# A decoder layer with product-key experts: how the indices of the first expert rows are made

## The reference, cut to what matters

```python
def reference(x, mem, ...):                       # x: 1 x 256 x 1024, float32
    h = rmsnorm(x, norm_mix);   x = x + hybrid_mixer(h, ...)            # 16 heads of attention, w_in, w_out
    h = rmsnorm(x, norm_xattn); x = x + memory_cross_attention(h, ...)  # w_xq, w_xk, w_xv, w_xo
    h = rmsnorm(x, norm_ffn);   x = x + peer_ffn(h, ...)
    return rmsnorm(x, norm_final)

def one_chunk(xc):                                # inside peer_ffn: 128 tokens
    qr = (xc @ w_query).reshape(C, PEER_HEADS, 2, half)        # 8 heads
    s1 = einsum('chd,hnd->chn', qr[:, :, 0], sub_keys_1)       # 128 keys a side
    s2 = einsum('chd,hnd->chn', qr[:, :, 1], sub_keys_2)
    v1, i1 = top_k(s1, 16);  v2, i2 = top_k(s2, 16)
    cand = v1[..., :, None] + v2[..., None, :]                 # 16 x 16 sums
    top_s, pos = top_k(cand, 16)
    eidx = take_along_axis(i1 * 128 + i2, pos)                 # 16 experts per head
    g = softmax(top_s)
    a = gelu(einsum('cd,chkd->chk', xc, expert_down[eidx]))
    return einsum('chk,chkd->cd', g * a, expert_up[eidx])
```

## Time and profile before

| | us |
|---|---|
| median of 3 runs | 937.75 (935.33 to 939.22) |
| the profiled execution's own time | 927.9 |
| its span, first to last instruction | 926.1 |
| PE busy | 815.2 |
| DVE busy | 556.4 |
| ACT busy | 443.6 |
| POOL busy | 242.6 |
| bytes moved by DMA | 316.33 MB |

### The profile page before, as it was taken

The page is one execution under the profiler, slowest core; times in us unless marked ns, Lnnn a source line. Parts: engine busy times, 40 slices in busy tenths (PEclk is TensorE's granted clock), DMA queues, the critical chain, the costliest instruction groups (busy, mean ns, idle before and its releaser), DMA issues.

```text
span 926.1 us, 9462 instructions
## 1 busy us (share of the span) xinstructions
PE 815.2 (88%) x3195; PEld 457.9 (49%) x3195; DVE 556.4 (60%) x1345; ACT 443.6 (48%) x1088; POOL 242.6 (26%) x267
## 2 busy tenths in 40 slices
PE   7999999999989899888898999977877788787875
PEld 7999986687555365343343455432322222232322
DVE  5555333213456776777767758776766766676543
ACT  5435564324134645664546545464453545445343
POOL 0000000000023333334334333433333333333430
PEclk9999999999999999999999999999999999999999
DMA  9896632061099999999999999999999999999995
GB/s 334 227 312 244 205 115 91 1 230 44 1 371 413 415 422 419 413 416 421 419 409 421 421 413 417 418 410 416 421 422 421 422 421 416 421 408 423 409 422 218
DMA packets 64339, 316.33 MB, mean 342 GB/s; under 512 B 7907, under 2 KB 12068, under 8 KB 31524
## 3 DMA queue, kind: packets, MB, share of 16 engines
q0 software_dynamic: 36864, 268.45, 70.1%
q1 hardware_dynamic: 26348, 45.70, 13.9%
q10 hardware_dynamic: 1080, 1.59, 1.1%
HBM read 313.10 MB, written 2.62 MB: 341 GB/s over the span
## 4 chain that ended last, share of the span: by engine, by line
PE 53%; DMA 29%; ACT 10%; DVE 6%; issue 2%; POOL 0%; SPq 0%; POOLq 0%
DMA qkvb<-in_expert_rows,expert_idx 22%; PE y L1311 14%; PE v_bank L1311 8%; DMA spare<-in_expert_rows,expert_idx 6%; PE h_psum L1087 5%; PE v_bank L1077 5%; PE a_bank L1077 4%; PE a_bank L1087 4%; PE v_bank L1087 3%; DVE qkvb L1017 3%; PE h_psum L1077 3%; ACT L722 2%; PE v_bank L1176 2%; ACT diag L729 2%; PE y L1197 1%
## 5 line engine op out<-in xcount | busy, mean ns | idle before, releaser
L554 POOL DMA_INDIRECT qkvb<-in_expert_rows,expert_idx x172 | 162.1, 942 | 530.3 <-DVE expert_idx L1000 256.8
L722 ACT ACTIVATE gelu<-dots,stat 128x1 f32<-128x1 f32 x256 | 75.1, 293 | 309.3 <-DVE dots L1017 308.7
L1311 PE MATMUL v_bank<-qkvb,diag 128*128 128x512 f32 x344 | 171.8, 630 | 45.5 <-ACT diag L729 45.5
L1311 PE MATMUL y<-qkvb,diag 128*128 128x512 f32 x344 | 161.8, 607 | 21.2 <-ACT diag L729 21.2
L1017 DVE CUSTOM_DVE_ANT_0 qkvb<-a_bank,qkvb 128x1024 f32<-128x1024 f32 x86 | 105.3, 1224 | 74.1 <-DMA qkvb<-in_expert_rows,expert_idx 74.1
L1017 DVE CUSTOM_DVE_ANT_0 qkvb<-h_psum,qkvb 128x1024 f32<-128x1024 f32 x86 | 105.1, 1223 | 60.3 <-DMA qkvb<-in_expert_rows,expert_idx 60.3
L1311 PEld LDWEIGHTS v_bank<-qkvb,diag 128*128 128x128 f32 x344 | 61.4, 194 | 155.4 <-ACT diag L729 105.1
L554 POOL DMA_INDIRECT spare<-in_expert_rows,expert_idx x84 | 79.0, 941 | 132.5 <-PE y L1311 65.9
L1311 PEld LDWEIGHTS y<-qkvb,diag 128*128 128x128 f32 x344 | 62.1, 191 | 100.6 <-issue 56.5
L729 ACT ACTIVATE diag<-ident,wgt 128x128 f32<-128x128 f32 x256 | 102.7, 401 | 8.3
L1311 PE MATMUL v_bank<-spare,diag 128*128 128x512 f32 x168 | 85.1, 635 | 20.5 <-ACT diag L729 20.5
(11 more groups left out here) (204 smaller groups left out, 1142.8 us busy)
## 6 DMA issues: line engine op xcount, KB each, us to landing
weights<-in_w_in SPq DMA_DIRECT2D x5, 2048.0 KB, 33.2
weights<-in_w_xk SPq DMA_DIRECT2D x2, 2048.0 KB, 17.4
weights<-in_w_xv SPq DMA_DIRECT2D x2, 2048.0 KB, 10.7
weights<-in_w_out SPq DMA_DIRECT2D x2, 2048.0 KB, 8.9
weights<-in_w_xq SPq DMA_DIRECT2D x2, 2048.0 KB, 8.5
weights<-in_w_xo SPq DMA_DIRECT2D x2, 2048.0 KB, 12.1
weights<-in_w_peer_query SPq DMA_DIRECT2D x2, 2048.0 KB, 16.5
qkvb<-in_expert_rows,expert_idx POOLq DMA_INDIRECT x172, 9.9
```

What stands on the lines that cost most here:

```text
L554: pool.indirect_dma_start(ROWS[n % NS], None, expert_rows, bass.IndirectOffsetOnAxis(ap=IDX[:, H % 3, k:k + 1], axis=0))\
L722: nc.scalar.activation(gel[:, i:i + 1], dots[:, i:i + 1], ACT.Gelu, scale=rms("root_p", n // SPT)).then_inc(gelu_done, 1)
L1311: ins = nc.tensor.matmul(YP[t][:, b * BLK:(b + 1) * BLK], diag[:, i, :], ROWS[i][:, D + b * BLK:D + (b + 1) * BLK], start=False, stop=n % ...
```

## The change

It has five parts. (1) The norm weights of the last norm are a sixth load into `grow`, and `pT` transposes `X[0]` itself; DVE multiplies by the weight columns as the transpose leaves its bank. `xg` and ACT's copy are gone. (2) A quarter of `wout(1, 1)` that stood between the two transposes stands behind the scores now, and the two `y_start` products change place. (3) `top_part` reads scores where they lie, without a copy, for all 16 heads. (4) For head 0 the places of the first eight sums are turned into indices before the other eight are looked for (`FIRST_TOP`), and the reciprocal of the norm moves behind them. (5) POOL waits for the first eight indices before row tile 0 and for the others before row tile 8. Token tile 1 gets part 1 too.

```diff
-    main += [("xo", 0, 0), ("oT", 1, 0), ("xg", 0, 0), ("oT", 1, 1), ("xo", 0, 1), ("xg", 0, 1), ("pT", 0, 0)]
-    main += rest[1][:1] + [("square_p", 0, 0), ("pT", 0, 1), ("start", 0, 0), ("wq_first", 0, 0), ("y_start", 0, 0),
-                           ("sc_first", 0, 0), ("sc_first", 0, 1), ("root_p", 0, 0), ("top", 0, 0), ("y_start", 0, 1)]
-    main += rest[1][1:] + [("wq", 0, 0), ("sc", 0, 0), ("sc", 0, 1)] + rest[0]
+    main += [("xo", 0, 0), ("oT", 1, 0), ("oT", 1, 1), ("xo", 0, 1), ("pT", 0, 0), ("y_start", 0, 0), ("square_p", 0, 0),
+             ("pT", 0, 1), ("start", 0, 0), ("wq_first", 0, 0), ("sc_first", 0, 0), ("sc_first", 0, 1),
+             ("y_start", 0, 1), ("root_p", 0, 0), ("top", 0, 0)]
+    main += rest[1] + [("wq", 0, 0), ("sc", 0, 0), ("sc", 0, 1)] + rest[0]
...
+    CHOICE = ("pairs", "ones", "picks", "experts")
+    FIRST_TOP = TOP[:8] + tuple("first " + part for part in CHOICE) + TOP[8:11] + tuple(
+        "last " + part for part in CHOICE) + TOP[15:]
...
-                if k == 0:
-                    pool.wait_ge(idx_ready, H + 1)
+                if n == 0:
+                    pool.wait_ge(idx_ready, 1)
+                elif n == 8 or n > 8 and k == 0:
+                    pool.wait_ge(idx_ready, H + 2)
...
-            for r in (4, 0, 3):
+            for r in (4, 0, 3, 5):
                 load_gain(act, r)
...
-                elif name == "pT":
-                    src = job(key)
-                    act.copy(HT[t][:, 4 * i:4 * i + 4, :], src[:, :].rearrange("p (c x) -> p c x", c=4))\
-                        .then_inc(a_free, 1)
...
+                    if name == "wq_first":
+                        act.wait_ge(sum_done, norm_n[0])
...
-                    for part in TOP:
-                        if part == "sums":
+                    for part in FIRST_TOP:
+                        if part == "sums out":
                             rstd(("root_p", 0, 0))
                         top_part(part, 0)
...
-                elif name == "xg":
-                    own = slice(i * BLK, (i + 1) * BLK)
-                    dve.wait_ge(ld_gffn, 16)
-                    dve.wait_ge(*freed(("xo", t, i)))
-                    nc.vector.tensor_tensor(HTpage[t][:, own], X[t][:, own], gffn[:, own], ALU.mult)\
-                        .then_inc(xs_done, 1)
+                elif name == "pT":
+                    gained(key, i, HT[t], 32)
...
+                side = [sc[:, s, :] if lo else scores[:, s * NKEY:(s + 1) * NKEY] for s in range(2)]
                 if part in ("keys", "more keys"):
                     if lo == 0:
                         top_n[0] = 0
-                        after(t_mark(nc.vector.tensor_copy(sc[:, :, :].rearrange("p a x -> p (a x)"), scores)))
...
                 elif name == "pT":
-                    pe.wait_ge(xs_done, XN[("xg", t, i)])
-                    transposes(key, HTpage[t], i)
+                    pe.wait_ge(*freed(("xo", t, i)))
+                    transposes(key, X[t], i)
                 elif name == "y_start":
-                    pe.wait_ge(v_free, VN[("xo", t, 1)] + 1)
+                    pe.wait_ge(*freed(("xo", t, i)))
```

More of the change, by code:

```diff
@@ L189, in hybrid_layer @@
               (122, ("sc", 1, 2)), (123, ("sc", 1, 3))]
-    OWN = ("root_x", "rstd_x", "xnorm", "xg", "square_p", "root_p", "rstd_p")
+    OWN = ("root_x", "rstd_x", "xnorm", "square_p", "root_p", "rstd_p")
     def after_slot(n, products):
@@ L284, in hybrid_layer @@
         skT = sb("subkeys_t", [P, PH, NKEY])
-        grow = PT[0:32, 0, 0:P]
-        gcol = sb("gain_cols", [P, 32])
+        grow = PT[0:40, 0, 0:P]
+        gcol = sb("gain_cols", [P, 40])
         wf = sb("w_forget", [P, KC, NH])
@@ L776, in gained @@
                                         src[:, :].rearrange("p (c x) -> p c x", c=4),
-                                        gain, ALU.mult).then_inc(v_free, 1)
+                                        gain, ALU.mult).then_inc(freed(key)[0], 1)
             def step(name, t, i):
@@ L939, in top_part @@
                 lo = 8 if part.startswith("more") else 0
+                ks = slice(0, PK)
+                if part.startswith(("first", "last")):
+                    ks = slice(0, 8) if part.startswith("first") else slice(8, PK)
+                    part = part.split()[1]
+                nk = ks.stop - ks.start
+                side = [sc[:, s, :] if lo else scores[:, s * NKEY:(s + 1) * NKEY] for s in range(2)]
                 if part in ("keys", "more keys"):
@@ L946, in top_part @@
                     for s in range(2):
-                        ins = nc.vector.max(kv[:, s, lo:lo + 8], sc[:, s, :])
+                        ins = nc.vector.max(kv[:, s, lo:lo + 8], side[s])
                         top_mark["keys", s] = t_mark(ins)
@@ L981, in top_part @@
                     after(top_mark["sum places"])
-                    t_mark(nc.vector.tensor_scalar(pab[:, 0, :], pos[:, :], 4, None, ALU.logical_shift_right))
-                    after(t_mark(nc.vector.tensor_scalar(pab[:, 1, :], pos[:, :], 15, None, ALU.bitwise_and)))
-                    top_mark[part] = t_mark(nc.vector.tensor_copy(pabf[:, :, :], pab[:, :, :]))
+                    t_mark(nc.vector.tensor_scalar(pab[:, 0, ks], pos[:, ks], 4, None, ALU.logical_shift_right))
+                    after(t_mark(nc.vector.tensor_scalar(pab[:, 1, ks], pos[:, ks], 15, None, ALU.bitwise_and)))
+                    top_mark[part] = t_mark(nc.vector.tensor_copy(pabf[:, :, ks], pab[:, :, ks]))
                 elif part == "ones":
@@ L994, in top_part @@
                         top_mark[part] = t_mark(nc.vector.tensor_tensor(
-                            hot[:, s, :, :], hot[:, s, :, :],
-                            kf[:, s, :].unsqueeze(1).broadcast_to([P, PK, PK]), ALU.mult))
+                            hot[:, s, ks, :], hot[:, s, ks, :],
+                            kf[:, s, :].unsqueeze(1).broadcast_to([P, nk, PK]), ALU.mult))
                 elif part == "experts":
                     after(top_mark["picks"])
-                    after(t_mark(nc.vector.tensor_reduce(picked[:, :, :], hot[:, :, :, :], AX.X, ALU.add)))
-                    nc.vector.scalar_tensor_tensor(out=IDX[:, H3, :], in0=picked[:, 0, :], scalar=float(NKEY),
-                                                   in1=picked[:, 1, :], op0=ALU.mult, op1=ALU.add)\
+                    after(t_mark(nc.vector.tensor_reduce(picked[:, :, ks], hot[:, :, ks, :], AX.X, ALU.add)))
+                    nc.vector.scalar_tensor_tensor(out=IDX[:, H3, ks], in0=picked[:, 0, ks], scalar=float(NKEY),
+                                                   in1=picked[:, 1, ks], op0=ALU.mult, op1=ALU.add)\
                         .then_inc(idx_ready, 1)
@@ L1127, in step @@
                     pe.wait_ge(id_ready, 1)
-                    pe.wait_ge(ld_gain, 16 * 5)
+                    pe.wait_ge(ld_gain, 16 * 6)
                     bank = bank_for(key)
-                    nc.tensor.transpose(bank[:, 0:32], grow[:, :], ident[0:32, 0:32]).then_inc(v_full, 1)
+                    nc.tensor.transpose(bank[:, 0:40], grow[:, :], ident[0:40, 0:40]).then_inc(v_full, 1)
                 elif name == "memT":
```

19 lines of the change are left out of this document (10 added, 9 removed).

## The result

The changed kernel takes 939.54 us (median of 20 runs, 933.73 to 947.01), the kernel before 934.52 us (median of 20 runs on the same chips). The ratio is 1.0058, interval 1.0038 to 1.0078: 0.58% slower. The time lies in the range that I gave (933.5 to 941.0), and that is luck. I had forecast + 0.3 us and no change that can be measured; it is + 5.0 us between the medians, with an interval clear of no change. The range was built around 937.75, the median of three runs of the kernel before; around the 934.52 of twenty it would lie 3.2 us lower and leave 939.54 out.

What follows compares the result with a forecast made beforehand. The prediction took the kernel as bound by the DMA engines' start, then a fixed number of bytes: + 0.6 for the later start, - 0.3 for the block beside row tiles, 937.75 + 0.3, about 938.0 us, range 933.5 to 941.0.

Steps and rivals of the forecast that it cites:

- What bounds the kernel: Whole kernel: time until the DMA engines start for good, then fixed bytes, 256 row tiles and two blocks of `w_peer_query`.
- The chain to the first indices: From DVE's addition to POOL's first issue: savings on PE and DVE bring row tile 0 4.0 us sooner, at 255.2.
- What PE pays: PE ahead of the expert phase: `wout(1, 1)` ends later, so block 1's issue, first dot and row tile 6 come 0.6 later.
- Where the stretch starts: Start of full DMA work: block 1's data come first, at 257.8, 0.6 us later than before.
- The 3.2 us: Row tile 0: its data begin 3.2 us after POOL's issue, at 258.4; bounded below by 1.8.
- the paragraph on what is hidden: Early expert phase: engines fed until 282.9, row tile 6's data at 279.8, so cover stays 3.1 us.
- One gain stays: the block now runs beside row tiles: Transfer of block 1: sharing with row tiles takes 5.0 us instead of 5.3, 0.3 saved, bounds 0 and 0.3.
- (a): Rival at the first index: the time goes with it, 937.75 - 4.0 = 933.75; chance 0.13.
- (b): Rival at the small loads: the sixth gain load lands late, end some 3 us later, 940.8; chance 0.06.
- (c): Rival at row tile data: they begin 1.8 us after issue, 937.25; no own chance, inside the 0.76 of conserved bytes.
- the likeliest case: Whole kernel: conserved bytes, about 938.0 us, 937.2 to 938.4 by the terms; chance 0.76.
- not named: Whole kernel: something the prediction did not name decides the time; chance 0.05.

Runs made afterwards that it cites:

- all16: Changed kernel with one wait undone, row tile 0 issued only when all 16 indices of head 0 are written: 1.0025 (1.0000 to 1.0049), 932.77 us.
- split_after: Changed kernel with block 1 of `w_peer_query` loaded in four parts, each once its quarter of `wout(1, 1)` is used: 1.0016 (0.9984 to 1.0049).
- the second: The changed kernel run again, unaltered, against the kernel before: 1.0088 (1.0054 to 1.0123), 939.36 us.
- early8_before: Kernel before with only parts 4 and 5 of the change (first eight indices first, POOL starts on them): 0.9984 (0.9956 to 1.0012).
- split_before: Kernel before with block 1 of `w_peer_query` loaded in four parts, each once its quarter of `wout(1, 1)` is used: 0.9993 (0.9965 to 1.0021).

## Why the prediction was right or wrong

**What bounds the kernel** was right: a fixed number of bytes behind the start of the DMA stretch. From 100 us behind the addition on both kernels move 408 to 422 GB/s in each stretch of 50 us, and the two groups of the table differ in the bytes moved in the first 67 us.

**The chain to the first indices** was right: 11.7 us from the addition to the first issue by my sum, 11.78 and 11.77 measured; 4.0 us sooner forecast, 3.9 measured. The half width of the three one-hot steps, for which I took 0.8, can be read now: two operations of 128 elements take 0.49 where two of 256 took 0.76.

**What PE pays** was right: SP's issue 12.5 us after the addition by my sum and 12.50 measured, the first dot + 0.59. That all this costs by itself about what I said (0.3 to 0.6) is compatible with all16 and not shown by it: + 0.5 us between medians, + 2.3 by the ratio, interval 0 to 4.6.

**Where the stretch starts** was right to a few tenths, but not by which transfer. Reckoned as in the prediction, 0.81 MB had moved by 264 us, at 410 GB/s 2.0 us: a start at 262.0, 14.3 us after the addition, as forecast (257.8 - 243.5; before 13.7). But the row tile's data come first, not the block's: 0.16 against 0.01 MB from 261 to 262, the first of them at 261.3, 1.8 us after POOL's issue. The 3.2 us that I had taken held only where the block was moving ahead of the rows. And it was the wrong question. I asked when the first byte flows. I did not ask when the last byte of the block lands.

**The step that failed** stands in the paragraph on what is hidden: "six row tiles and both blocks are 10.5 MB, at 417 GB/s 25.1 us ... The cover is 3.1 us, as before, because both ends move alike". It treats all bytes as one heap, and asks only whether the engines have work until the data of row tile 6 come. They had: 396 GB/s from 280 to 290, and row tile 6 was issued after 33.00 us, 0.1 from the forecast. The sum has no term for row tile 7, nor for a wait of PE for the block. PE doesn't wait for the heap but for one transfer in it. In the kernel before that transfer had the engines alone; the change puts 6.3 MB of row tiles beside it, and the queues share by packets of unlike size. I had said "One gain stays: the block now runs beside row tiles"; this is the very thing that costs the time. The consequence runs in a ring: late block, PE stands 3.9 us and works at half its clock behind that, the products of row tile 1 on PE end late (its dots are in time), row tile 7 is issued 6.1 us late, and the engines, which I had said would be fed, fall dry.

The rows for it were there. The quarter of `wq(0, 1)` starts on PE 20.1 us after the block's issue in the kernel before (275.54 - 255.41; it landed after 7.8), and the queues of the earlier trace rows gave a packet of 8 KB against one of 2 KB (0.26 MB in 32, 0.57 MB in 292). Shared in turn, the block gets 2 / (2 + 8) of 417 GB/s, some 83 GB/s: in the time of the six row tiles, 6.3 MB at 334 GB/s or 19 us, that is 1.6 MB, and the rest follows alone in 1.3. With some 2 us until its first data that is an estimate of 22 us against the 20.1 that PE leaves it; 24.1 were measured.

**The rivals.** (a), the full 4 us, did not happen; nor did its half where the block is in time (split_after). (b), the late gain load, did not happen: PE's transpose of the gains starts at 6.02, before 6.11. (c) can't be told from the likeliest case by the time; the trace has the 1.8 us that it named, but slow first microseconds (164 and 260 GB/s from 261 to 263) used up the gain. The slower side won by a mechanism that I had not named, and to which I had given, under "not named", 5 in 100. Of what I wrote would prove me wrong, the engines falling dry did show, though just outside the stretch that I named: the hole begins at 290, 42 us after the addition, and my stretch (270 to 285) ended 285 - 243.50 = 41.5 us behind it.

**What stays open.** The cost of the change is 5 us by the medians of the first comparison and 6.3 in the second (939.36 to 933.07); the bytes of the first 67 us say 6.7. Part of the difference lies in single executions. From the addition to the last instruction the profiled ones took 682.6 us before and 692.4 and 690.1 in the changed kernel, but also 688.9 in early8_before, whose runs are no slower than the kernel before. One pair of rows in which they differ, first of the kernel before, then of the changed one, eight products each:

```profile
312.57 3.70 PE L1311 MATMUL y<-qkvb,diag 128*128 128x512 f32 x8 [3.37 <-ACT diag L729]
```

```profile
323.71 6.57 PE L1317 MATMUL y<-qkvb,diag 128*128 128x512 f32 x8 [3.51 <-ACT diag L733]
```

Around the second the clock is 0.66 (320 to 330), and the changed kernel has another hole, 353 GB/s from 330 to 340, where the kernel before has 424. early8_before (6.52 us) and split_before (5.40), which are no slower, have it too, all16 (3.70) has not. How much of the change's loss hangs on it is not known. Nor is it known why the later places of `wq(0, 1)` cost time by themselves.

## What to carry to other kernels

When an edit moves the start of one transfer past another's, list each transfer that shares the engines at that time and ask when it lands and who waits for it; "the engines are fed" answers only half. A queue with large packets leaves little to one with small packets (here four fifths to one), so a weight block that PE needs soon should be issued ahead of a burst of gathers, or before it in parts; here 1.4 us of lead were enough, and 0.7 us behind the first gather it took three times as long to land as with 3 us of lead. And where a ring of buffers is released by PE, indices that come sooner bring nothing until PE's part comes sooner too.

## What the runs showed of the hardware

Which of two issues comes first is worth 9 us of landing time for a block of 2.1 MB when they are less than 1 us apart, and 16 us over 4 us of lead: 7.8 us with a lead of 3 us, 11.5 with 1.4, 15.0 with 0.3, 24 with -0.7 (one execution each, three of the last). That the curve is so steep I had not expected.

A wait of 3.9 us cost PE more than its length. The granted clock had fallen just before it, behind an earlier stand of 3.01 us, and stayed low through it: from 282 to 286 it was 0.50 (the 1.2 GHz level), and the 16 products behind the wait took 3.78 us. In the kernel before they took 2.55, where the clock was coming back, and the next quarter 1.95 at a clock of 1.00. The same 3.01 us left the clock at 1.00 in early8_before. The window of the changed kernel:

```profile
282.00:286.00 4.00, 1.61 (x7) 1.61 (x8) 3.89 (x13) 1.80 (x6) 0.00 (x0) 0.50 1.07 404
```

And a fall to half of the clock can come with PE busy all the time (10.00 of 10 us at a clock of 0.50, 220 to 230 us, first profile), in some executions of a kernel and not in others. Two single executions are better compared from an instruction behind such a stretch than from the start of the span.
